# Residual projections with one 512-column product for both operand parts

## Chip, core and metric

The kernel runs on one core of a Trainium2 chip. The metric is device time in microseconds (us) for one execution; the kernel before takes 1901.9 us (median of 3 runs, 1900.17 to 1902.33).

## The reference, cut to what matters

The reference is two transformer blocks, one after the other, in float32, on a sequence of 256 tokens with 1024 channels. The first has three mixing branches, merged and projected back onto `x`; the second, of two layers, has SwiGLU feed-forward parts, an RWKV-7 time mix in layer 0, a gated MLP with a token mix in layer 1, and a memory cross-attention in each layer. Five of its matrix products end in an addition to the residual stream `x`, and these five are what the change touches:

```
x = x + merged @ w_out                      # first block        stage w_out
x = x + (y * g) @ rwkv_w_o                  # layer 0, RWKV      stage rw_o
x = x + attention_out @ xattn_wo[0]         # layer 0, memory    stage xo0
x = x + (u * sv) @ gmlp_w_o                 # layer 1, gMLP      stage gm_o (2048 rows deep)
x = x + attention_out @ xattn_wo[1]         # layer 1, memory    stage xo1
```

All weights are 1024 x 1024 but that of `gm_o`, which is 2048 x 1024. Each of the five is followed by an RMS norm of the new `x` and a projection of the result: a feed-forward part after `w_out`, `xo0` and `xo1`, the query projection of the memory attention after `rw_o` and `gm_o`.

## The kernel before

**Split precision.** TensorE multiplies in the type fp32r. So each float32 operand is held as two parts, a high one (rounded to fp32r) and a low one (the rest), and a product of weight w and activation a is three products: w high with a high, w high with a low, w low with a high (`split_mm`, L307). ScalarE makes the high part of a weight piece (`high`, L1592, recorded as L1602, tile `wh`), VectorE the low part (`low`, L2419, recorded as L2428, tile `wl`).

**Weight stream.** All weights come as one stream of 1 MB blocks, loaded by the sync engine (SP) into two raw slots; a slot is loaded again once VectorE has split both halves of it. A block is two pieces of 4 x 256 columns. There are four slots of split pieces: ScalarE writes piece p + 4 when TensorE has finished piece p (semaphore `piece_done`), and TensorE starts a piece when its low part is done (`low_done`, `piece`, L319). Each engine's order of work is written out by hand.

**Tiling.** Activations lie with channels on the 128 partitions, as 8 tiles of 256 tokens in a page of 2048 columns. A projection makes its 1024 output channels in four blocks q = 0 to 3 of two output tiles (j = 0, 1) by 256 tokens, into one PSUM bank of 512 columns. A residual projection walks over the 8 k tiles of the depth (16 for `gm_o`), four in each piece; per k and j there are three products of 256 columns, all recorded at L311. So a piece is 24 products, a block 48 (96 in `gm_o`), a stage 192 (384). In the first block TensorE waits for the operand in quarters of two k tiles (`operand_part`, L433). The banks 0 to 3 go round; `bank_free` (L325) waits until the engine that reads a bank has emptied it (`u_evac`).

**The other form.** In the SwiGLU stages the activation's two parts lie next to each other, and `wide_block` (L382) uses one product of 512 columns for w high with both parts (L398), and one of 256 columns for w low with the high part (L401), added in PSUM to the second half. Two output tiles then take two banks, and VectorE adds the two halves of a bank (L2976). In a whole piece 8 products of 512 columns are issued and then 8 of 256; behind a name's first piece they come in halves, 4 and 4.

**Around a residual stage.** VectorE's `residual` (L2519) does for each block q: split the weights of the block two ahead, wait until block q is made, add the bank to `x` (L2529; in `gm_o` L3361). For q = 3 it first makes the low quarters 0 and 1 of the next stage's operand (`late_quarters`, L2492, recorded as L2501) and a part of the norm's sum of squares (L2473, L2474), then adds block 3, then makes quarters 2 and 3. ScalarE makes the high quarters of that operand (`late_quarter`, L1678) when the blocks of `x` that it reads are added. TensorE's next stage waits for these quarters in turn.

Of the kernel before, what the change touches and what calls it, by code (L numbers as in the profile page):

```python
# [24 lines left out]
F32R = mybir.dt.float32r  # L25
# [5 lines left out]
P = 128  # L31
D = 1024
KT = D // P
T = 256
# [21 lines left out]
N_FFN = 5  # L56
AHEAD = 2
N_PAGES = 16
COL_EPS, COL_GN_EPS = 40, 41
HIDDEN_PAGES = {1: (0, 9, 10, 11, 14, 15), 2: (3, 6, 7, 8, 10, 11)}  # L60

# [11 lines left out]
for _name, _n in PARAMS:  # L73
# [16 lines left out]

SEGMENTS = [
    ("mem_k", 2, 2), ("mem_v", 2, 2), ("w_in", 40, 40), ("na_o", 4, 2), ("ca_o", 4, 2), ("hg_o", 4, 4),
    ("w_out", 4, 4), ("ffn0", 22, 33), ("ffn1", 44, 33), ("mem2_k", 4, 4), ("rw_k", 4, 4), ("mem2_u", 1, 1), ("lora", 0, 1),
    ("rw_r", 4, 5), ("lora2", 0, 1), ("mem2_v", 3, 3), ("rw_v", 4, 4), ("rw_o", 4, 4), ("xq0", 4, 4), ("xo0", 4, 4),
    ("ffn2", 44, 33), ("ffn3", 44, 33), ("gm_u", 2, 2), ("gm_v", 8, 8), ("gm_w", 6, 6), ("gm_o", 4, 8),
    ("xq1", 4, 4), ("xo1", 4, 4), ("ffn4", 44, 33),
]
W_IN_ORDER = [*range(8, 16), *range(0, 4), *range(20, 28), *range(4, 8), *range(16, 20), *range(32, 40), *range(28, 32)]
WOVEN = 18
# [76 lines left out]
def build(nc, a):  # L176

    ctx = ExitStack()
    with ctx:
        def sb(name, shape):  # L180
            return ctx.enter_context(nc.sbuf_tensor(name, shape, F32))

        t = Bag()


        def both(name, pages=1):
            at = -(-nc.sbuf_base // 32) * 32
            plain = sb(name, [P, pages * FP])
            split = [nc.alloc_sbuf_tensor_at(f"{name}_r{i}", [P, FP], F32R, offset=at + 4 * FP * i)[:, :]
                     for i in range(pages)]  # L190
# [113 lines left out]
def tensor_program(pe, t, s):  # L304
# [77 lines left out]
    def wide_block(n, bank, b, name=None, between=lambda: None):  # L382

        bank_free(n + 1)
        for hf in range(2):
# [3 lines left out]
            for run in ((0, 1), (2, 3)) if name and hf else (range(4),):  # L389
                for part in range(2):  # L390
                    for kk in run:
# [3 lines left out]
                        for j in range(2):  # L395
# [7 lines left out]
            mm.then_inc(s["piece_done"], 1)  # L403

    def token_block(n, bank, b, act, name=None):
        for hf in range(2):
# [339 lines left out]
    project("w_out", (t.page_r[11], t.page_r[10]), name="merged")  # L746


    ffn(0, "ffn0", "ffn0")
# [411 lines left out]
    project("rw_o", (t.page_r[10], t.page_r[7]), name="rw_o")  # L1161


    def memory_heads(i):
# [35 lines left out]
    def memory_attention(i, name):  # L1200
# [12 lines left out]
            turn(h)  # L1213
            mix(h - 1)
        mix(XA_H - 1)
        for k in range(4):
            n = SEG[f"xo{i}"] + k
            bank_free(n)
            for hf in range(2):
                w = piece(BLK[f"xo{i}"] + k, hf)  # L1220
                for kk in range(4):
                    c = 4 * hf + kk
                    if k == 0 and c % 2 == 0:
                        pe.wait_ge(s["att_low"], NA_H + CA_H + XA_H * i + c // 2 + 1)
                    for j in range(2):
                        mm = split_mm(ps[:, n % BANKS, j * T:(j + 1) * T],
                                      [x[:, kk * 256 + j * P:kk * 256 + (j + 1) * P] for x in w],
                                      [t.page_r[q][:, c * T:(c + 1) * T] for q in (2, 1)],
                                      start=c == 0 and j == 0, stop=c == KT - 1)
                mm.then_inc(s["piece_done"], 1)  # L1230

    memory_attention(0, "x0")
    swiglu(2, "ffn2", "ffn2")
# [37 lines left out]
    for q in range(4):  # L1271
        n, b = SEG["gm_o"] + q, BLK["gm_o"] + 2 * q
        bank_free(n)
        for k4 in range(4):
            w = piece(b + k4 // 2, k4 % 2)
            for j in range(2):
                for kk in range(4):
                    k = 4 * k4 + kk
                    if q == 0 and j == 0:
                        operand_part(f"gm{k // KT}", k % KT)  # L1280
                    mm = split_mm(ps[:, n % BANKS, j * T:(j + 1) * T],
                                  [x[:, kk * 256 + j * P:kk * 256 + (j + 1) * P] for x in w],
                                  [t.page_r[first + k // KT][:, k % KT * T:(k % KT + 1) * T] for first in (10, 7)],
                                  start=k4 == 0 and j == 0 and kk == 0, stop=k == 2 * KT - 1)
            mm.then_inc(s["piece_done"], 1)
    memory_attention(1, "x1")
    swiglu(4, "ffn4", "ffn4")
    for q in range(4):
# [106 lines left out]
def split_pair(t, first, second, m):  # L1395

    base = t.pages[:, first:first + m]
    return bass.AP(tensor=base.tensor, offset=base.offset,
                   ap=[list(base.ap[0]), [2 * m, 512 // m], [second - first + m, 2], [1, m]])


def strided_pair(t, first, second):
# [151 lines left out]
def norm_table(t, s):  # L1554
# [3 lines left out]
    rows = {  # L1558
        "mem": (t.page[0], (s["mem_in"], 16, 0), ("mem_norm", 0), t.page[1]),
        "mix0": (x, (s["x_in"], 16, 0), ("norm_mix", 0), low),  # L1560
        "ffn0": (x, (s["u_evac"], seg["w_out"] + 2, 2), ("norm_ffn", 0), h),
        "ffn1": (x, (s["x_up"], 2, 2), ("gain_fin", 0), h),
        "mix1": (x, (s["x_up"], 4 + 2, 2), ("mix_norm_2", 0), h),
        "mem2": (t.page[6], (s["mem2_in"], 16, 0), ("mem_norm_2", 0), t.page[6]),
        "x0": (x, (s["u_evac"], seg["rw_o"] + 2, 2), ("xattn_norm_2", 0), h),
        "ffn2": (x, (s["u_evac"], seg["xo0"] + 2, 2), ("ffn2_norm_2", 0), h),
        "ffn3": (x, (s["x_up"], 8 + 2, 2), ("ffn1_norm_2", 8), h),
        "mix2": (x, (s["x_up"], 12 + 2, 2), ("mix_norm_2", 8), low),
        "x1": (x, (s["u_evac"], seg["gm_o"] + 2, 2), ("xattn_norm_2", 8), h),
        "ffn4": (x, (s["u_evac"], seg["xo1"] + 2, 2), ("ffn2_norm_2", 8), h),  # L1570
        "fin2": (x, (s["x_up"], 16 + 2, 2), ("final_norm_2", 0), h),
    }
    return rows
# [839 lines left out]
def vector_program(dve, t, s):  # L2413
# [105 lines left out]
    def residual(seg, first=0, n=4, then=None):  # L2519

        for k in range(first, first + n):
            n_ = SEG[seg] + k
            if k < 3 or not then:
# [4 lines left out]
            c = slice(k * 512, (k + 1) * 512)  # L2528
            tt(t.x[:, c], ps[:, n_ % BANKS, :], t.x[:, c], ALU.add).then_inc(s["u_evac"], 1)  # L2529
            if then and k == 3:  # L2530
                late_quarters(then, (2,))

    def ffn_residual(f_, scale, then=None, after=None):
        for q in range(4):
# [818 lines left out]
            mixed_quarter(q)  # L3353
    mixed_low(7)
    for q in range(4):
        c = slice(q * 512, (q + 1) * 512)
# [4 lines left out]
        tt(t.x[:, c], ps[:, (SEG["gm_o"] + q) % BANKS, :], t.x[:, c], ALU.add).then_inc(s["u_evac"], 1)  # L3361
    late_quarters("x1", (2,))
    memory_attention(1, "ffn4", BLK["gm_o"] + 7)
    def final_part(q):
# [202 lines left out]
```

## Time and profile before

| | |
|---|---|
| runs | 1902.33, 1900.17, 1901.9 us |
| profiled execution | 1902.15 us, of which 1900.4 us span |
| TensorE products | 1856.1 us, 98%, 15872 instructions |
| weight loads | 1716.6 us, 90% |
| VectorE | 1369.4 us, 72% |
| ScalarE | 1075.6 us, 57% |
| mean granted TensorE clock | 0.998 of 2.4 GHz |
| read from HBM | 310.50 MB, 164 GB/s over the span |

The span runs from the first to the last instruction on the core. Times of products are modelled at their ends, so their starts are the ones to read: the time from one start to the next is what a product costs in a row of them.

### The profile page before, as it was taken

How to read it: one execution, taken by the hardware profiler on the slowest of the kernel's cores; microseconds unless marked ns; L12 is line 12 of the kernel's file. 1: busy time of each engine (PE TensorE's matmuls, PEld its weight loads, DVE VectorE, ACT ScalarE, POOL GpSimd, SP SyncE). 2: the span in 40 equal slices, each digit the busy share in tenths (PEclk: the TensorE clock that was granted, in tenths of full speed). 3: DMA queues.
4: the chain of work that ended last, by engine and by line, in shares of the span. 5: the costliest groups of instructions: out<-in, count | busy, mean ns of one | idle time of the engine just before them, and what ended most of it. 6: DMA issues, size and time to landing. Idle time of an engine off the chain costs nothing.

```text
span 1900.4 us, 37888 instructions
## 1 busy us (share of the span) xinstructions
PE 1856.1 (98%) x15872; PEld 1716.6 (90%) x15872; DVE 1369.4 (72%) x1808; ACT 1075.6 (57%) x1443; POOL 45.0 (2%) x42
## 2 busy tenths in 40 slices
PE   7999998999999999999998999999999999999998
PEld 7998998899998888999887998888888889998887
DVE  6687589777778877698755667766776657658764
ACT  6576576755556554468543555545554574556553
POOL 0000000000000000000142000000000000000000
PEclk9999999999999999999999999999999999999999
DMA  6844333355554455544400535554555554525553
GB/s 226 242 180 154 135 133 113 141 191 177 193 183 155 177 196 185 180 150 163 149 25 8 196 116 194 186 191 177 200 183 194 178 186 169 179 110 199 179 198 111
DMA packets 52335, 313.66 MB, mean 165 GB/s; under 512 B 13536, under 2 KB 13792, under 8 KB 14944
## 3 DMA queue, kind: packets, MB, share of 16 engines
q1 hardware_dynamic: 51760, 308.42, 45.8%
q10 hardware_dynamic: 432, 3.15, 0.4%
q8 instruction: 112, 1.84, 0.4%
q14 instruction: 31, 0.25, 0.0%
HBM read 310.50 MB, written 1.05 MB: 164 GB/s over the span
## 4 chain that ended last, share of the span: by engine, by line
PE 75%; DVE 14%; ACT 4%; issue 4%; DMA 2%; DVEq 0%; ACTq 0%; SPq 0%
PE ps L311 28%; PE ps L398 17%; PE ps L401 9%; PE ps L535 9%; DVE wl L2428 5%; PE ps L532 4%; ACT wh L1602 2%; DVE pages L2950 2%; DMA raw<-in_stream 2%; PE ps L922 1%; PE ps L937 1%; DVE pages L3050 1%; DVE pages L2516 1%; PE ps L1194 1%; DMA pages<-in_mem 0%
## 5 line engine op out<-in xcount | busy, mean ns | idle before, releaser
L2428 DVE TENSOR_TENSOR wl<-raw,wh 128x1024 fp32r<-128x1024 f32 x576 | 696.4, 1226 | 331.6 <-ACT wh L1602 327.6
L1602 ACT ACTIVATE wh<-raw 128x1024 fp32r<-128x1024 f32 x575 | 597.7, 1054 | 417.6 <-PE ps L311 143.2
L311 PE MATMUL ps<-norm_r,wh 128*128 128x256 f32 x2336 | 430.1, 285 | 0.3 <-DVE norm_r L2445 0.2
L311 PEld LDWEIGHTS ps<-norm_r,wh 128*128 128x128 f32 x2336 | 365.9, 192 | 3.3 <-issue 1.8
L311 PE MATMUL ps<-pages_r,wh 128*128 128x256 f32 x1776 | 343.8, 286 | 16.1 <-DVE wl L2428 13.7
L398 PE MATMUL ps<-norm_r,wh 128*128 128x512 f32 x1408 | 355.2, 394 | 1.9 <-DVE norm_r L2501 1.7
L311 PE MATMUL ps<-norm_r,wl 128*128 128x256 f32 x1184 | 334.9, 283 | 0.0
L311 PEld LDWEIGHTS ps<-pages_r,wh 128*128 128x128 f32 x1776 | 285.1, 193 | 20.2 <-DVE wl L2428 11.8
L398 PEld LDWEIGHTS ps<-norm_r,wh 128*128 128x128 f32 x1408 | 253.6, 189 | 47.7 <-issue 1.9
L311 PE MATMUL ps<-pages_r,wl 128*128 128x256 f32 x976 | 277.0, 284 | 0.0
L311 PEld LDWEIGHTS ps<-norm_r,wl 128*128 128x128 f32 x1184 | 227.0, 192 | 0.0
L401 PEld LDWEIGHTS ps<-norm_r,wl 128*128 128x128 f32 x1408 | 193.5, 191 | 14.2
L401 PE MATMUL ps<-norm_r,wl 128*128 128x256 f32 x1408 | 197.7, 283 | 0.0
L311 PEld LDWEIGHTS ps<-pages_r,wl 128*128 128x128 f32 x976 | 188.2, 193 | 0.0
L535 PE MATMUL ps<-pages_r,wh 128*128 128x512 f32 x704 | 177.7, 392 | 0.0
L535 PEld LDWEIGHTS ps<-pages_r,wh 128*128 128x128 f32 x704 | 126.0, 189 | 22.1
L532 PEld LDWEIGHTS ps<-pages_r,wl 128*128 128x128 f32 x704 | 97.1, 190 | 7.6
L532 PE MATMUL ps<-pages_r,wl 128*128 128x256 f32 x704 | 99.4, 282 | 0.0
L311 PE MATMUL ps<-wh,norm_r 128*128 128x512 f32 (+1 forms) x256 | 71.8, 367 | 0.0
L311 PE MATMUL ps<-work_r,wh 128*128 128x256 f32 x272 | 70.6, 284 | 0.0
L2516 DVE TENSOR_TENSOR work<-work,rstd 128x512 f32<-128x512 f32 x88 | 60.6, 689 | 9.6 <-ACT work L2095 2.9
L311 PEld LDWEIGHTS ps<-wh,norm_r 128*128 128x128 f32 x256 | 45.5, 189 | 8.8 <-issue 1.8
(341 smaller groups left out, 1918.1 us busy)
## 6 DMA issues: line engine op xcount, KB each, us to landing
raw<-in_stream SPq DMA_DIRECT2D x287, 1024.0 KB, 4.8
pages<-in_rpb SPq DMA_DIRECT2D x32, 64.0 KB, 6.2
pages<-in_mem SPq DMA_DIRECT2D x2, 512.0 KB, 6.4
raw<-in_stream SPq DMA_DIRECT2D x2, 512.0 KB, 8.1
x<-in_x SPq DMA_DIRECT2D x1, 1024.0 KB, 12.0
pages<-in_mem ACTq DMA_DIRECT2D x1, 1024.0 KB, 5.0
pages<-in_gmlp_b ACTq DMA_DIRECT2D x1, 1024.0 KB, 4.4
pages<-in_gmlp_w ACTq DMA_DIRECT2D x1, 1024.0 KB, 8.2
```

The source lines that it names most:

```text
L311: mm = pe.matmul(out, left, right, start=start and q == 0, stop=stop and q == 2, skip_group_check=True)
L398: mm = pe.matmul(ps[:, bank + j, :], wh[:, cols], t.norm_r[:, 2 * k * T:2 * (k + 1) * T], start=k == 0, stop=False, skip_group_check=True)
L401: mm = pe.matmul(ps[:, bank + j, T:2 * T], wl[:, cols], t.sq_r[:, k * T:(k + 1) * T], start=False, stop=k == KT - 1, skip_group_check=True)
L532: mm = pe.matmul(ps[:, bank, T:2 * T], w[1][:, cols], hid[:, 0:T], start=False, stop=k == HT - 1, skip_group_check=True)
L535: mm = pe.matmul(ps[:, bank, :], w[0][:, cols], hid, start=k == 0, stop=False, skip_group_check=True)
L922: mm = pe.matmul(ps[rows[1 - par], g % 2, at_:at_ + CH], level[rows[par], at_:at_ + CH], inv[rows[par], x:x + CH], start=True, stop=True)
L937: mm = pe.matmul(ps[rows[par ^ turned], bank + turned, (4 * e + u) * CH:(4 * e + u + 1) * CH], left, right, start=True, stop=True)
L1194: mm = pe.matmul(ps[:, memory_bank(i, "out", h), c * T:(c + 1) * T], t.page[15][:, at_:at_ + P], memory_turned(t, h)[:, mb * T:(mb + 1) * ...
L1602: f(t.wh[(2 * b0 + hf) % PIECE_SLOTS][:], t.raw[b0 % 2][:, hf * 1024:(hf + 1) * 1024], ACT.Copy).then_inc(s["high_done"], 1)
L2428: tt(t.wl[i][:], t.raw[b0 % 2][:, hf * 1024:(hf + 1) * 1024], t.wh[i][:].bitcast(F32), ALU.subtract).then_inc(s["low_done"], 1)
L2516: return tt(out.rearrange("p (n t) -> p n t", n=n), in_, t.rstd[:, :].unsqueeze(1).broadcast_to([P, n, T]), ALU.mult)
L2950: ins = stt(o, i_, w, o, ALU.mult, ALU.add)
```

## The change

In the five residual stages, blocks q = 0, 1 and 2 take the two-bank form. A block now uses banks n and n + 1, one for each output tile. For each k and j, one product of 512 columns has the high weight tile and both parts of the activation (its moving operand is a view of two pages, low or high part first by page number); then products of 256 columns with the low weight tile and the high part go into the second half of the bank. Block q = 3 keeps one bank and the three products of 256 columns, with j as the outer loop. VectorE adds the first halves of both banks to `x`, and behind that (it waits for its own result) the second halves; block 3 is added as before. `SEGMENTS` counts 8 banks for a stage in place of 4, and what waits for `u_evac` counts double. The pages' aliases of type fp32r are joined where a view must span two pages; no address moves.

```diff
+    def residual_piece(n, b, hf, first, pages, start, stop, ready=lambda k: None):
+        w = piece(b, hf)
+        runs = ((0, 1), (2, 3)) if first else (range(4),)
+        for run in runs:
+            for low_part in range(2):
+                for kk in run:
+                    k = 4 * hf + kk
+                    if not low_part:
+                        ready(k)
+                    for j in range(2):
+                        cols, bank = slice(kk * 256 + j * P, kk * 256 + (j + 1) * P), n % BANKS + j
+                        if low_part:
+                            mm = pe.matmul(ps[:, bank, T:2 * T], w[1][:, cols], t.page_r[pages[0]][:, k * T:(k + 1) * T],
+                                           start=False, stop=stop and k == KT - 1, skip_group_check=True)
+                        else:
+                            mm = pe.matmul(ps[:, bank, :], w[0][:, cols], both_parts(t, pages, k), start=start and k == 0,
+                                           stop=False, skip_group_check=True)
+        mm.then_inc(s["piece_done"], 1)
...
+    def residual(seg, parts, ready):
+        for q in range(4):
+            n, b = SEG[seg] + 2 * q, BLK[seg] + len(parts) * q
+            bank_free(n + 1)
+            for at_, pages in enumerate(parts):
+                for hf in range(2):
+                    start, stop = at_ == hf == 0, at_ == len(parts) - 1
+                    if q < 3:
+                        residual_piece(n, b + at_, hf, q == 0, pages, start, stop,
+                                       (lambda k: ready(KT * at_ + k)) if q == 0 else (lambda k: None))
+                    else:
+                        last_residual_piece(n, b + at_, hf, pages, start, stop)
...
+def both_parts(t, pages, k):
+    first, second = sorted(pages)
+    base = t.page_r[first][:, k * T:(k + 1) * T]
+    return bass.AP(tensor=base.tensor, offset=base.offset, ap=[list(base.ap[0]), [(second - first) * FP, 2], [1, T]])
...
-        "ffn0": (x, (s["u_evac"], seg["w_out"] + 2, 2), ("norm_ffn", 0), h),
+        "ffn0": (x, (s["u_evac"], seg["w_out"] + 4, 4), ("norm_ffn", 0), h),
...
+    def added(seg, q):
+        n, c = SEG[seg] + 2 * q, slice(q * 512, (q + 1) * 512)
+        if q < 3:
+            made, x = ps[:, n % BANKS:n % BANKS + 2, :], tiles(t.x[:, c], 2)
+            link(tt(x, made[:, :, 0:T], x, ALU.add))
+            tt(x, made[:, :, T:2 * T], x, ALU.add).then_inc(s["u_evac"], 2)
+        else:
+            tt(t.x[:, c], ps[:, n % BANKS, :], t.x[:, c], ALU.add).then_inc(s["u_evac"], 2)
```

## Rows read from the trace of the kernel before

**Rows 1.** The page's totals: busy us, share of the span, instructions.

```profile
span 1900.4 us, 37888 instructions
...
PE 1856.1 (98%) x15872; PEld 1716.6 (90%) x15872; DVE 1369.4 (72%) x1808; ACT 1075.6 (57%) x1443; POOL 45.0 (2%) x42
```

**Rows 2.** Chain of waits through stage `xo0`: start, us, engine and line, count.

```profile
1105.10 23.03 PE ps L311 x192
```

**Rows 3.** Busy us (count) of PE, PEld, DVE, ACT, POOL; PEclk, DMA share, GB/s.

```profile
380.10:403.90 23.80, 23.80 (x200) 23.80 (x200) 16.29 (x22) 11.53 (x16) 0.00 (x0) 1.00 0.52 191
1045.60:1064.00 18.40, 18.40 (x156) 18.40 (x155) 11.27 (x14) 8.64 (x12) 0.00 (x0) 1.00 0.62 232
1104.90:1127.90 23.00, 23.00 (x193) 22.97 (x193) 12.39 (x16) 10.31 (x14) 0.00 (x0) 1.00 0.33 116
...
1140.00:1180.00 40.00, 40.00 (x229) 35.14 (x229) 31.62 (x38) 23.97 (x32) 0.00 (x0) 1.00 0.55 197
600.00:603.00 3.00, 3.00 (x12) 2.61 (x12) 2.84 (x4) 0.91 (x3) 0.00 (x0) 0.50 0.00 0
```

**Rows 4.** TensorE's timeline in a SwiGLU stage: start, us (modelled end), instruction, count.

```profile
1142.38 2.00 PE L398 MATMUL ps<-norm_r,wh 128*128 128x512 f32 x8
1144.22 1.12 PE L401 MATMUL ps<-norm_r,wl 128*128 128x256 f32 x8
1145.18 2.00 PE L398 MATMUL ps<-norm_r,wh 128*128 128x512 f32 x8
...
1147.97 0.40 PE L398 MATMUL ps<-norm_r,wh 128*128 128x512 f32 x1
```

**Rows 5.** The same timeline behind `xo0`, where pieces come in halves.

```profile
1130.76 1.09 PE L398 MATMUL ps<-norm_r,wh 128*128 128x512 f32 x4
...
1132.16 1.09 PE L398 MATMUL ps<-norm_r,wh 128*128 128x512 f32 x4
...
1133.57 0.63 PE L398 MATMUL ps<-norm_r,wh 128*128 128x512 f32 x2
```

**Rows 6.** The same timeline before and in the first block of `rw_o`.

```profile
1034.14 3.70 PE L1157 MATMUL ps<-norm,const 128*128 128x512 f32 x8
1037.68 1.84 PE L317 MATMUL ps<-zrow 128*128 128x128 bf16 x30
1040.26 0.47 PE L311 MATMUL ps<-pages_r,wh 128*128 128x256 f32 x2 [0.74 <-DVE pages_r L2451]
...
1042.18 0.51 PE L311 MATMUL ps<-pages_r,wh 128*128 128x256 f32 x2 [0.27 <-DVE pages_r L2451]
...
1044.21 0.47 PE L311 MATMUL ps<-pages_r,wh 128*128 128x256 f32 x2 [0.33 <-DVE pages_r L2451]
```

**Rows 7.** VectorE's groups: the addition of two half banks; busy us, mean ns, idle.

```profile
L2976 DVE TENSOR_TENSOR work<-ps,work 128x512 f32<-128x512 f32 x44 | 30.3, 689 | 26.7 <-ACT work L2075 26.7
```

**Rows 8.** VectorE's timeline before `rw_o`: the second instruction waits for the first.

```profile
1036.76 0.69 DVE L3231 TENSOR_TENSOR pages<-pages 128x512 f32<-128x512 f32 x1 [0.19 <-ACT pages L2292]
1037.48 0.69 DVE L3232 TENSOR_TENSOR pages<-pages 128x512 f32<-128x512 f32 x1
```

**Rows 9.** VectorE's timeline in `xo0`, from the addition of block 1 on.

```profile
1118.88 0.68 DVE L2529 TENSOR_TENSOR x<-ps,x 128x512 f32<-128x512 f32 x1
1120.68 1.23 DVE L2428 TENSOR_TENSOR wl<-raw,wh 128x1024 fp32r<-128x1024 f32 x1 [1.12 <-ACT wh L1602]
...
1124.64 0.68 DVE L2529 TENSOR_TENSOR x<-ps,x 128x512 f32<-128x512 f32 x1
...
1128.17 0.69 DVE L2529 TENSOR_TENSOR x<-ps,x 128x512 f32<-128x512 f32 x1 [0.20 <-PE ps L311]
1128.78 0.87 DVE L2501 SCALAR_TENSOR_TENSOR norm_r<-x,param,norm_r 128x256 fp32r<-128x256 f32 x2
1129.84 0.88 DVE L2501 SCALAR_TENSOR_TENSOR norm_r<-x,param,norm_r 128x256 fp32r<-128x256 f32 x2 [0.19 <-ACT norm_r L1678]
```

**Rows 10.** VectorE's timeline in `gm_o`: the addition of block 3.

```profile
1641.53 0.69 DVE L3361 TENSOR_TENSOR x<-ps,x 128x512 f32<-128x512 f32 x1 [0.80 <-PE ps L311]
```

More of the change, by code:

```diff
@@ L58 @@
 N_PAGES = 16
+ALIASES = [(0, 1), (1, 2), *((i, 1) for i in range(3, 7)), (7, 5), *((i, 1) for i in range(12, N_PAGES))]
 COL_EPS, COL_GN_EPS = 40, 41
@@ L92 @@
     ("mem_k", 2, 2), ("mem_v", 2, 2), ("w_in", 40, 40), ("na_o", 4, 2), ("ca_o", 4, 2), ("hg_o", 4, 4),
[L93 to L96, printed above, removed]
+    ("w_out", 8, 4), ("ffn0", 22, 33), ("ffn1", 44, 33), ("mem2_k", 4, 4), ("rw_k", 4, 4), ("mem2_u", 1, 1), ("lora", 0, 1),
+    ("rw_r", 4, 5), ("lora2", 0, 1), ("mem2_v", 3, 3), ("rw_v", 4, 4), ("rw_o", 8, 4), ("xq0", 4, 4), ("xo0", 8, 4),
+    ("ffn2", 44, 33), ("ffn3", 44, 33), ("gm_u", 2, 2), ("gm_v", 8, 8), ("gm_w", 6, 6), ("gm_o", 8, 8),
+    ("xq1", 4, 4), ("xo1", 8, 4), ("ffn4", 44, 33),
 ]
@@ L188, in both @@
             plain = sb(name, [P, pages * FP])
-            split = [nc.alloc_sbuf_tensor_at(f"{name}_r{i}", [P, FP], F32R, offset=at + 4 * FP * i)[:, :]
-                     for i in range(pages)]
+            split = []
+            for first, n in ALIASES if pages > 1 else ((0, 1),):
+                alias = nc.alloc_sbuf_tensor_at(f"{name}_r{first}", [P, n * FP], F32R, offset=at + 4 * FP * first)
+                split += [alias[:, i * FP:(i + 1) * FP] for i in range(n)]
             return plain, split
@@ L403, in wide_block, with last_residual_piece @@
             mm.then_inc(s["piece_done"], 1)
+    def residual_piece(n, b, hf, first, pages, start, stop, ready=lambda k: None):
[16 more added lines that the diff above has]
+        mm.then_inc(s["piece_done"], 1)
+    def last_residual_piece(n, b, hf, pages, start, stop):
+        w = piece(b, hf)
+        for j in range(2):
+            for kk in range(4):
+                k = 4 * hf + kk
+                mm = split_mm(ps[:, n % BANKS, j * T:(j + 1) * T], [x[:, kk * 256 + j * P:kk * 256 + (j + 1) * P] for x in w],
+                              [t.page_r[q][:, k * T:(k + 1) * T] for q in pages],
+                              start=start and j == 0 and kk == 0, stop=stop and k == KT - 1)
+        mm.then_inc(s["piece_done"], 1)
+    def residual(seg, parts, ready):
[10 more added lines that the diff above has]
+                        last_residual_piece(n, b + at_, hf, pages, start, stop)
     def token_block(n, bank, b, act, name=None):
@@ L745, in tensor_program @@
     project("hg_o", (t.page_r[6], t.page_r[13]), name="hg")
-    project("w_out", (t.page_r[11], t.page_r[10]), name="merged")
+    residual("w_out", ((11, 10),), lambda k: operand_part("merged", k))
     ffn(0, "ffn0", "ffn0")
@@ L1160, in tensor_program @@
     idle_products(4, 30)
-    project("rw_o", (t.page_r[10], t.page_r[7]), name="rw_o")
+    residual("rw_o", ((10, 7),), lambda k: operand_part("rw_o", k))
     def memory_heads(i):
@@ L1215, in memory_attention, with ready @@
         mix(XA_H - 1)
[L1216 to L1230, printed above, removed]
+        def ready(c):
+            if c % 2 == 0:
+                pe.wait_ge(s["att_low"], NA_H + CA_H + XA_H * i + c // 2 + 1)
+        residual(f"xo{i}", ((2, 1),), ready)
     memory_attention(0, "x0")
@@ L1270, in tensor_program @@
         mix_quarters(MIX_BEHIND[k - 1])
[L1271 to L1285, printed above, removed]
+    residual("gm_o", ((10, 7), (11, 8)), lambda k: operand_part(f"gm{k // KT}", k % KT))
     memory_attention(1, "x1")
@@ L1564, in norm_table @@
         "mem2": (t.page[6], (s["mem2_in"], 16, 0), ("mem_norm_2", 0), t.page[6]),
-        "x0": (x, (s["u_evac"], seg["rw_o"] + 2, 2), ("xattn_norm_2", 0), h),
-        "ffn2": (x, (s["u_evac"], seg["xo0"] + 2, 2), ("ffn2_norm_2", 0), h),
+        "x0": (x, (s["u_evac"], seg["rw_o"] + 4, 4), ("xattn_norm_2", 0), h),
+        "ffn2": (x, (s["u_evac"], seg["xo0"] + 4, 4), ("ffn2_norm_2", 0), h),
         "ffn3": (x, (s["x_up"], 8 + 2, 2), ("ffn1_norm_2", 8), h),
         "mix2": (x, (s["x_up"], 12 + 2, 2), ("mix_norm_2", 8), low),
-        "x1": (x, (s["u_evac"], seg["gm_o"] + 2, 2), ("xattn_norm_2", 8), h),
-        "ffn4": (x, (s["u_evac"], seg["xo1"] + 2, 2), ("ffn2_norm_2", 8), h),
+        "x1": (x, (s["u_evac"], seg["gm_o"] + 4, 4), ("xattn_norm_2", 8), h),
+        "ffn4": (x, (s["u_evac"], seg["xo1"] + 4, 4), ("ffn2_norm_2", 8), h),
         "fin2": (x, (s["x_up"], 16 + 2, 2), ("final_norm_2", 0), h),
@@ L2517, in scaled, with residual @@
                   t.rstd[:, :].unsqueeze(1).broadcast_to([P, n, T]), ALU.mult)
[L2519 to L2523, printed above, removed]
+    def added(seg, q):
[6 more added lines that the diff above has]
+            tt(t.x[:, c], ps[:, n % BANKS, :], t.x[:, c], ALU.add).then_inc(s["u_evac"], 2)
+    def residual(seg, then):
+        for k in range(4):
+            if k < 3:
                 low(BLK[seg] + k)
@@ L2527, in residual @@
             dve.wait_ge(s["piece_done"], 2 * (BLK[seg] + k) + 2)
[L2528 to L2531, printed above, removed]
+            added(seg, k)
+        late_quarters(then, (2,))
     def ffn_residual(f_, scale, then=None, after=None):
@@ L3355, in vector_program @@
     for q in range(4):
-        c = slice(q * 512, (q + 1) * 512)
         lows("gm_o", 2 * q, 2 if q < 3 else 1)
@@ L3360, in vector_program @@
         dve.wait_ge(s["piece_done"], 2 * (BLK["gm_o"] + 2 * q) + 4)
-        tt(t.x[:, c], ps[:, (SEG["gm_o"] + q) % BANKS, :], t.x[:, c], ALU.add).then_inc(s["u_evac"], 1)
+        added("gm_o", q)
     late_quarters("x1", (2,))
```

## The prediction

> **What bounds the kernel now.** I read the page's totals first, then the chain of waits inside one of the five stages that change, then busy time by stretch, then that stage's VectorE timeline. In the totals TensorE is busy 98% of the span and weight loads 90% [rows 1]. That alone does not name the limit of a stage, so the chain is asked for the second residual projection of the memory attention: from its first product to the next stage it is one piece, 192 products in 23.03 us, with no other engine in it [rows 2]. So a product of 256 columns costs 23.03 / 192 = 120 ns, and everything else in that stage lies under TensorE. The stretches say the same of the other stages, of which three stand in the rows and the two others are alike: TensorE is busy in all of each stretch, VectorE in 54 to 68% of it, the DMA engines in 33 to 62%, and the granted clock is 1.00 [rows 3]. The reader is to see there that 1 us taken from TensorE's stream in such a stage is 1 us of the time, as long as whoever feeds the next stage does not become late.
>
> **What the change removes.** A block has two pieces (half blocks), each with 4 k tiles and 2 output tiles: 8 triples of 256-column products. The new piece has 8 products of 512 columns and 8 of 256. The columns streamed are the same (6144 a piece); 8 products and 8 weight loads go. Before, a piece is 24 x 0.120 = 2.88 us. The kernel already holds pieces of the new form, in the wide blocks of the SwiGLU stages: two in a row start at 1142.38, 1145.18 and 1147.97, so one is 5.59 / 2 = 2.795 us [rows 4]. A whole piece therefore gains 0.085 us. The first block of a stage is issued in halves (4 + 4 products, for two k tiles); the same form stands at 1130.76, 1132.16 and 1133.57, 1.405 us a half, 2.81 us a piece [rows 5], a gain of 0.07 us.
>
> Pieces: four stages have three changed blocks of two pieces (2 in halves, 4 whole); the gMLP output, with twice the depth, has 12 (4 in halves, 8 whole). Together 12 x 0.07 + 24 x 0.085 = 0.84 + 2.04 = 2.88 us. In the first block of the RWKV output TensorE waits three times for VectorE's operand quarters, at 1040.26, 1042.18 and 1044.21 [rows 6]. What it gains in the first two quarters (0.035 us each) is waited away: 0.07 us less. Sum: 2.8 us.
>
> The Trainium skill (TensorE: Matmul & The Clock Gate, section Back-to-back issue gap) gives a product its columns at the clock and a constant of about 2.5 ns. By that rule, as an estimate, a triple would save one constant, and 288 triples 0.7 us. The trace doesn't agree: 120 ns for 256 columns [rows 2] and 230 ns for 512 (1142.38 to 1144.22, eight of them) [rows 4] save 2 x 120 - 230 = 10 ns a triple.
>
> One thing no row shows: the new 512-column operand is two runs of 256 from two pages, where the wide blocks read one run. Bounds: if the jump is free, 230 ns; if each run pays as a product of its own, 2 x 120 = 240 ns, and the gain is nil. Further out stand the 512-column products of plain fp32, 8 from 1034.14 to 1037.68, 442 ns each [rows 6]. I take 230: the nearest row has the same width, type and weights, and only one jump in 512 columns is new. Below 230 I see no reason.
>
> **What it adds on VectorE.** Three blocks of a stage get a second addition: 15 in all. A two-bank addition in this view is in the trace 44 times at 689 ns [rows 7], as long as the old one. The first of the pair is waited for by the second; such a pair starts 1037.48 - 1036.76 = 0.72 us apart [rows 8]. So each block costs VectorE 0.72 us more, 10.8 us in all. After blocks 0 and 1 of a stage it lies in an idle time of 1.12 us before the next weight split (L2428 at 1120.68 after block 1; after block 0 the same) [rows 9], so it costs nothing. Without that cover it would delay a split whose piece TensorE reaches only three pieces later.
>
> After block 2 it counts. Behind that addition, in VectorE's order, stand the low quarters 0 and 1 of the next operand, a part of the norm's sum, block 3's addition, then quarters 2 and 3, for which TensorE's next stage waits. In the memory attention's stage VectorE was free for block 3's addition 0.20 us before 1128.17 [rows 9]. Block 2 now ends 2 x 0.07 + 4 x 0.085 = 0.48 us earlier, and with it the split and the addition. So VectorE is free at 1128.17 - 0.20 - 0.48 + 0.72 = 1128.21, 0.04 us later than before on the clock. Quarter 2, ready before at 1128.78 + 0.87 = 1129.65, is ready at 1129.69. TensorE needs it at the first half of the second piece, 1130.76 [rows 5], now 0.48 earlier: 1130.28. The cover shrinks from 1.11 to 0.59 us and holds. Quarter 3 is needed 1.40 us later and is ready 1.07 us later: 0.92 left. The other stages have the same 0.20 us or more; in the gMLP output VectorE idles 0.80 us there [rows 10] and TensorE's block ends 0.96 us earlier, so the addition still waits for TensorE.
>
> **What it adds in waits.** A changed block takes two of four banks, so block 2 waits for block 0's additions, block 3 for block 1's, and the next stage's first wide block for block 2's. Worked out in the same stage: block 1's additions end at 1118.88 - 0.31 + 1.40 = 1119.97 (0.31 is the gain of two blocks), and block 3 starts at 1105.10 + 17.28 - 0.48 = 1121.90 [rows 2, 9]. That is 1.9 us of room; block 0 to 2 has 1.8, block 2 to the next stage 1.9. Nothing on TensorE stands still for it. Weights, DMAs and the q = 3 block keep their instructions; SP's loads move earlier with the splits, and the DMA share of at most 0.62 [rows 3] has room.
>
> **Sum.** The profiled execution: 1902.15 us, 1900.4 span and 1.75 around it. 1902.15 - 2.8 = 1899.35. It stood 0.25 above the median of the runs shown (1901.9), so the forecast is **1899.1 us**. That is 0.15%; a measurement of this kernel tells about 0.2%, 3.8 us, from no change.
>
> **The rivals.**
> - Only columns count, or each run of the operand pays as a product: 8 x 240 + 8 x 120 is the old 2.88 us a piece, gain nil, 1901.9. For it: equal columns, and no row of a two-run operand. Against: rows 4. Chance 0.14.
> - Slower: the two-run operand costs more than two products. It decides from 240 ns on; from 253 ns it is slower by 0.2% (288 x 0.013 = 3.8 us). At 260 ns it costs 288 x 0.020 = 5.8 us, 1907.7. For it: only that no row excludes it, with 442 ns as the far end [rows 6]. Against: every 512-column product of this type in the trace runs at 230. Chance 0.07.
> - The hand-over becomes late: if the additions out of two half banks took 1.23 us each (the split's duration [rows 9]), VectorE would be late by another 1.1 us, 0.51 past the cover. In four stages that is 2.0 us, leaving 0.8: 1901.1. Against: rows 7. Chance 0.07.
> - Weight loads are the limit, and each of the 288 removed frees 120 ns: 34.6 us, 1867.3. For it: 90% in [rows 1] and loads in all of each stage's time [rows 3]. The Trainium skill (Perfetto Trace Analysis, section Identifying the Most-Contended Engine) judges TensorE by weight-load share rather than by matmul share. Against: with a third fewer loads the wide piece still takes 2.795, not 16 x 0.120 = 1.92 us, and in its stretch loads take 35.14 of 40 us [rows 3, 4]. Chance 0.05.
>
> One further risk is inside the range: the granted clock was 0.50 from 600 to 603 us, after a wait of TensorE [rows 3]. Such a stretch falling elsewhere, or not at all, moves the time by a microsecond or two.
>
> **How the numbers follow.** The forecast has 0.67. Its own range is 1898.0 to 1900.6, by the spread of the runs before (1900.17 to 1902.33); some 0.12 of the 0.67 falls under 1898.1, which is 0.2% faster. The range for 8 in 10 reaches over the two cases without much gain: 1897.3 to 1902.4. Faster by over 0.2%: 0.12 + 0.05 = 0.17. Slower: 0.07. Within: 0.76.
>
> **What would show it.** In the profile after: 512-column products of the new lines 230 ns apart; a whole changed piece 2.80 us and a stage of four blocks 0.48 us shorter (gMLP 0.96); 15 more additions of 0.69 us, each 0.72 behind its first half; VectorE idle before block 3's addition near zero in four stages; TensorE's next stage starting without a wait for quarter 2 or 3. The prediction is wrong if the two-run product is 240 ns or more, or if a wait of TensorE for the normalised operand (L2501) appears behind a residual stage.

## The result: 0.1 to 0.2% slower, and the profile after

The changed kernel took 1906.6 us in the median of eight runs (1902.3 to 1907.5), beside 1901.7 for the kernel before on the same chip: ratio 1.0019, 95% interval [1.0010, 1.0028]. Eleven more runs, on another occasion, gave 1903.5 us (1901.8 to 1907.2): ratio 1.0010 [1.0001, 1.0019]. The forecast was 1899.1, with 1897.3 to 1902.4 for 8 in 10: both medians lie outside, and the sign is wrong.

First the page of the changed kernel: span, and busy us, share and instructions of each engine.

```profile
span 1904.4 us, 37347 instructions
...
PE 1852.1 (97%) x15584; PEld 1700.3 (89%) x15584; DVE 1379.1 (72%) x1823; ACT 1075.6 (56%) x1443; POOL 45.1 (2%) x42
```

288 products and 288 weight loads are gone and 15 additions have come; TensorE is busy 4 us less than in [rows 1], yet the span is 4 us longer. So the time was lost where TensorE is idle. Before looking there, the changed stage itself, which answers [rows 2]: the chain of waits of the changed kernel through `xo0` (start, us, engine and line, count).

```profile
1111.14 0.93 PE ps L424 x4
...
1116.73 1.84 PE ps L424 x8
1118.57 0.95 PE ps L421 x8
1119.52 1.84 PE ps L424 x8
...
1127.90 5.76 PE ps L314 x48
1133.66 1.84 PE ps L401 x8
...
1136.45 0.93 PE ps L401 x4
```

The 512-column products over two pages (L424) are 230 ns each, the 256-column ones (L421) 119; a whole changed piece is 1119.52 - 1116.73 = 2.79 us, three changed blocks take 1127.90 - 1111.14 = 16.76 us instead of 3 x 5.76 = 17.28. Nothing but TensorE is in the chain. The next rows answer [rows 9]: VectorE's timeline at the end of the same stage.

```profile
1130.17 0.68 DVE L2555 TENSOR_TENSOR x<-ps,x 128x512 f32<-128x512 f32 x1
1130.96 0.69 DVE L2556 TENSOR_TENSOR x<-ps,x 128x512 f32<-128x512 f32 x1
...
1134.21 0.69 DVE L2558 TENSOR_TENSOR x<-ps,x 128x512 f32<-128x512 f32 x1
1134.81 0.88 DVE L2532 SCALAR_TENSOR_TENSOR norm_r<-x,param,norm_r 128x256 fp32r<-128x256 f32 x2
1135.88 0.88 DVE L2532 SCALAR_TENSOR_TENSOR norm_r<-x,param,norm_r 128x256 fp32r<-128x256 f32 x2 [0.19 <-ACT norm_r L1709]
```

The halves are added 0.79 us apart (forecast 0.72), block 3's addition has no idle time ahead of it, quarter 2 is ready at 1134.81 + 0.88 = 1135.69, and TensorE comes to it at 1136.45. So the stage goes as forecast (the cover of quarter 2 is 0.76 us, forecast 0.59). What was not forecast stands in the RWKV stage, which the change does not touch: TensorE's waits from 930 to 1050 us (line, releaser, us in total, times, longest), first the kernel before, then the changed one.

```profile
PE ps L1096 <- issue: 1.4, 1, 1.4
PE ps L311 <- DVE pages_r L2451: 1.3, 3, 0.7
PE ps L1029 <- issue: 1.1, 2, 0.8
PE ps L937 <- issue: 1.1, 1, 1.1
PE ps L922 <- issue: 1.0, 4, 0.3
...
```

```profile
PE ps L970 <- issue: 3.4, 5, 2.3
PE ps L1144 <- issue: 2.7, 2, 1.4
PE ps L985 <- issue: 2.3, 2, 1.3
PE ps L424 <- DVE pages_r L2482: 1.0, 2, 0.7
...
PE ps L1077 <- issue: 0.3, 1, 0.3
...
```

"issue" is time in which the engine waited for nothing that the profile shows. It was 4.6 us before (L1096, L1029, L937, L922) and is 8.7 us after, in the same code (L922 has become L970, L937 L985, L1096 L1144). The longest, in the changed kernel's timeline:

```profile
988.59 0.24 PE L970 MATMUL ps<-pages,norm 64*64 64x64 f32 x1
991.11 0.86 PE L970 MATMUL ps<-pages,norm 64*64 64x64 f32 x23 [2.29 <-issue]
```

What happens in it is in the DMA view of 988 to 992 us (queue, kind: packets, MB, share of 16 engines):

```profile
q1 hardware_dynamic: 32, 0.13, 8.0%
q8 instruction: 1, 0.02, 1.4%
```

A block of instructions is fetched: one transfer of 16,384 bytes, 256 instructions of 64 bytes, on a queue of its own. I took every such fetch of TensorE's queue from the trace, and every gap above 0.65 us between the starts of two products from 924 us to `rw_o`, and counted where the product behind the gap stands in TensorE's program (its place modulo 256). Listed are the gap's end, its length, the time from the start of the last fetch to that end (us), and the place.

```
before    924.16 0.97  4.67  (waits for wl)
          956.85 1.27  2.34  203    1008.43 1.04  2.39  205    1033.17 1.61  2.41  205
changed   925.99 0.96 24.80  (waits for wl)
          959.64 1.54  2.36  203     991.11 2.52  2.21  204     995.10 1.18  2.39  205
         1036.85 1.55  2.36  205    1040.33 1.60  2.34  205
```

But for the wait for a low weight tile at 924, every gap ends 2.2 to 2.4 us after a fetch began, and stands at places 203 to 205: a place that comes once in 256 instructions. I take it for the boundary where one block ends and the next begins. (It need not be place 0: the count starts at the kernel's first instruction, and that need not start a block.) They sum to 3.92 us before and 8.39 after, 4.47 more; the stage itself (from the 36 idle products ahead of it to the 30 ahead of `rw_o`, whose rows follow for the changed kernel) takes 198.65 us instead of 194.05: 4.60 more.

```profile
845.49 2.18 PE L320 MATMUL ps<-zrow 128*128 128x128 bf16 x36
...
1044.14 1.84 PE L320 MATMUL ps<-zrow 128*128 128x128 bf16 x30
```

In the kernel before these are 843.63 (a row like the first) and 1037.68 [rows 6].

### The profile page after: what moved, and what is told of

Same layout as the page of the kernel before. It is cut to its first block, busy times and chain, and to the rows that moved or that the text cites. A ratio compares the mean times of both kernels' runs of the same rounds, so it can differ in the third digit from the quotient of the medians.

```text
span 1904.4 us, 37347 instructions
## 1 busy us (share of the span) xinstructions
PE 1852.1 (97%) x15584; PEld 1700.3 (89%) x15584; DVE 1379.1 (72%) x1823; ACT 1075.6 (56%) x1443; POOL 45.1 (2%) x42
## 4 chain that ended last, share of the span: by engine, by line
PE 72%; DVE 15%; ACT 5%; issue 4%; DMA 3%; DVEq 0%; SPq 0%; ACTq 0%
PE ps L314 20%; PE ps L401 17%; PE ps L404 9%; PE ps L583 9%; DVE wl L2459 6%; PE ps L580 4%; PE ps L424 3%; DMA raw<-in_stream 3%; ACT wh L1633 2%; PE ps L421 2%; DVE pages L2988 2%; PE ps L970 1%; PE ps L985 1%; DVE pages L3088 1%; PE ps L1242 1%
## 5 line engine op out<-in xcount | busy, mean ns | idle before, releaser
L314 PE MATMUL ps<-pages_r,wh 128*128 128x256 f32 x1200 | 239.2, 287 | 16.8 <-DVE wl L2459 15.9
L314 PEld LDWEIGHTS ps<-pages_r,wh 128*128 128x128 f32 x1200 | 195.1, 193 | 20.1 <-DVE wl L2459 14.1
L314 PE MATMUL ps<-pages_r,wl 128*128 128x256 f32 x688 | 195.5, 284 | 0.0
L583 PE MATMUL ps<-pages_r,wh 128*128 128x512 f32 x704 | 177.7, 392 | 0.0
L583 PEld LDWEIGHTS ps<-pages_r,wh 128*128 128x128 f32 x704 | 126.0, 189 | 22.1
L314 PEld LDWEIGHTS ps<-pages_r,wl 128*128 128x128 f32 x688 | 132.9, 193 | 0.0
L580 PEld LDWEIGHTS ps<-pages_r,wl 128*128 128x128 f32 x704 | 97.1, 190 | 7.6
L580 PE MATMUL ps<-pages_r,wl 128*128 128x256 f32 x704 | 99.4, 282 | 0.0
L424 PE MATMUL ps<-pages_r,wh 128*128 128x512 f32 x288 | 75.0, 395 | 1.4 <-DVE pages_r L2482 1.4
```

The source lines that it names most:

```text
L314: mm = pe.matmul(out, left, right, start=start and q == 0, stop=stop and q == 2, skip_group_check=True)
L424: mm = pe.matmul(ps[:, bank, :], w[0][:, cols], both_parts(t, pages, k), start=start and k == 0, stop=False, skip_group_check=True)
L580: mm = pe.matmul(ps[:, bank, T:2 * T], w[1][:, cols], hid[:, 0:T], start=False, stop=k == HT - 1, skip_group_check=True)
L583: mm = pe.matmul(ps[:, bank, :], w[0][:, cols], hid, start=k == 0, stop=False, skip_group_check=True)
```

## The experiments

**Theory 1 (places).** TensorE's instructions come in blocks of 16,384 bytes. The 48 products that leave `w_out` are 96 instructions (a weight load and a product each), so all the code behind lies 96 places earlier against the block boundaries. The RWKV stage's dense small products meet the boundaries at worse points. **Theory 2 (the additions).** VectorE's additions, the waits for banks or the transfers that start earlier cost it. **Theory 3 (chance).** The clock and the transfers vary from run to run; nothing of the kernel is behind it.

The Trainium skill (Runtime: NRT & Kernel Launch, section Instruction fetch mechanics) tells of such blocks: 16 KiB, 256 instructions, which the sequencer fetches over a DMA queue of its own while it runs the one before. By it 96 places are three eighths of a block; the traces agree with the size (16,384 bytes a fetch).

Each trace is divided at the two rows of idle products shown above: A is the time up to the first, B the RWKV stage between them, C the rest of the span. Differences are against the profiled run of the kernel before (843.63, 194.05, 862.72 us).

| kernel | median us | ratio, 95% interval | A, us | B, us | C, us |
|---|---|---|---|---|---|
| changed | 1906.6 | 1.0019 [1.0010, 1.0028] | +1.86 | +4.60 | -2.46 |
| changed, again (e5) | 1903.5 | 1.0010 [1.0001, 1.0019] | -0.17 | +5.68 | -2.51 |
| before, moved by 160 (e1) | 1907.3 | 1.0031 [1.0020, 1.0043] | +2.05 | +4.20 | -0.05 |
| before, moved by 256 (e2) | 1914.4 | 1.0067 [1.0053, 1.0081] | +14.51 | -0.32 | -0.09 |
| changed, moved back by 96 (e3) | 1898.6 | 0.9981 [0.9972, 0.9990] | -0.59 | +0.18 | -2.49 |
| four later stages alone (e4) | 1899.3 | 0.9990 [0.9981, 0.9999] | -0.02 | -0.03 | -2.55 |
| `w_out` alone (e6) | 1906.4 | 1.0023 [1.0014, 1.0033] | +0.23 | +4.98 | -0.01 |
| changed, 96 waits in one place (e7) | 1908.0 | 1.0030 [1.0018, 1.0042] | +8.36 | -0.23 | -2.53 |
| changed, loops on block starts (e8) | 1904.1 | 1.0011 [1.0002, 1.0020] | -0.89 | +5.33 | -2.54 |
| changed, 84 idle products (e9) | 1899.2 | 0.9987 [0.9978, 0.9996] | -1.50 | +0.55 | -1.25 |
| changed, 68 idle products (e10) | 1899.4 | 0.9989 [0.9980, 0.9998] | -1.62 | +0.71 | -2.49 |
| changed, 100 idle products (e11) | 1902.6 | 1.0008 [0.9999, 1.0017] | -2.31 | +2.90 | -1.99 |
| before, 164 idle products (e12) | 1904.8 | 1.0016 [1.0006, 1.0025] | -0.45 | +2.32 | -0.07 |

**e1, e2: the code moved, without the change.** Two fulfilled waits ahead of a product of `w_out` add one instruction.

```diff
+    def pad():
+        for _ in range(min(1, pads[0])):      # e2: min(2, pads[0])
+            pe.wait_ge(s["consts_in"], 16)
+            pe.wait_ge(s["ones_in"], 16)
+            pads[0] -= 1
...
+            pad()                             # in split_mm, ahead of each product
...
+    pads[0] = 160                             # e2: 256
     project("w_out", (t.page_r[11], t.page_r[10]), name="merged")
```

> The kernel before, with the whole computation as it was, and 160 waits that are long fulfilled put between the products of the w_out stage on TensorE's queue: the TensorE program behind w_out then lies at the same places of its 16 KB fetch blocks as in the changed kernel. Theory 1 (the changed kernel lost its time because its TensorE code lies otherwise against the fetch blocks, above all in the RWKV stage): slower than before by 3 to 6 us, 1905 to 1908 us, and TensorE's waits for nothing in that stage grow from some 3.5 us to 8 us. Theory 2 (the added work of VectorE, the banks and the operand handed over cost it): the same as before within 1 us. Theory 3 (chance of the clock and of the transfers, nothing of the kernel): the same as before within 1 us.

> The kernel before with 256 such waits in the w_out stage, which is one whole fetch block: the code behind it lies where it lay against the blocks. It shows what the waits themselves cost. Theories 1, 2 and 3 all say the same as before, within 0.7 us; were it slower by 3 us, the first experiment would say nothing of places.

The two rows of e1 (the first pair) and of e2:

```profile
845.68 2.18 PE L326 MATMUL ps<-zrow 128*128 128x128 bf16 x36
1043.93 1.84 PE L326 MATMUL ps<-zrow 128*128 128x128 bf16 x30
...
858.14 2.18 PE L326 MATMUL ps<-zrow 128*128 128x128 bf16 x36
1051.87 1.84 PE L326 MATMUL ps<-zrow 128*128 128x128 bf16 x30
```

e1 is slower by 5.4 us with the old computation. Some 1.5 us of that fall in `w_out` itself, where the waits were added (24.51 us from its first product to the next stage's, instead of 23.04); the 4.20 us of B, where nothing was added, are what theory 1 says. Its gaps are four of the changed kernel's five (960.13, 991.32, 1036.64, 1040.11; 2.36 to 2.41 us after a fetch began, places 203 to 205). They sum to 6.23 us, 2.3 more than before. The rest of the 4.20 is in the windows behind the gap at 991.32 (busy TensorE us and count, granted clock, DMA share, GB/s):

```profile
990.00:992.00 2.00, 0.68 (x15) 0.86 0.00 0
992.00:994.00 2.00, 2.00 (x44) 0.50 0.04 8
994.00:996.00 2.00, 2.00 (x84) 0.78 0.00 0
```

The granted clock is 0.50, the lower of the two levels (1.2 GHz), in the middle window, and in parts of the two beside it: 2 x (0.14 + 0.50 + 0.22) = 1.7 us are lost there. The trace of the changed kernel itself shows no such stretch in this stage; that of e5 does, behind its gap at 957.89:

```profile
958.00:960.00 2.00, 1.64 (x35) 0.68 0.00 0
960.00:962.00 2.00, 2.00 (x47) 0.50 0.00 0
962.00:964.00 2.00, 2.00 (x132) 0.97 0.00 0
```

e8 has such a stretch too, behind a gap of 3.03 us (granted clock 0.62 from 990 to 992 us, 0.52 from 992 to 994). So in three traces a gap was followed by a second toll; the traces of the changed kernel and of e6, with gaps of up to 2.5 us, have none, and what decides it was not tested. Of the first eight runs of the changed kernel the four with a mean clock of 0.996 took 1907.0 to 1907.5 us.

e2 missed: it should have been as fast as before and was 12.5 us slower. The three parts show why it still serves: all of it is in A, where two added instructions a product were more than the stage hides, and the stage that is moved by one whole block keeps its time (-0.32). The prediction for the stage holds, the one for the sum fell.

**e3, e4, e6: moved back, and the change in parts.** e3 puts 96 such waits into the changed `w_out`. e4 and e6 compute the named stages as before and add their blocks once:

```diff
+APART = ('w_out',)                            # e6: ('rw_o', 'xo0', 'gm_o', 'xo1')
...
-                    if q < 3:
+                    if seg in APART:
+                        plain_piece(...)      # triples of 256-column products in one bank
+                    elif q < 3:
                         residual_piece(...)
...
-        if q < 3:
+        if q < 3 and seg not in APART:
             made, x = ps[:, n % BANKS:n % BANKS + 2, :], tiles(t.x[:, c], 2)
```

> The changed kernel with 96 such waits in its w_out stage: these fill the place of the 96 TensorE instructions that the change took out there, so that all from the end of w_out to rw_o (the RWKV stage among it) lies in the fetch blocks as before. Theory 1: the RWKV stage takes its old time and the sum comes out at 1898 to 1901 us, faster than before by 1 to 4 us. Theory 2: as the changed kernel, 1905 to 1907.5 us. Theory 3: anywhere between, without a shift of the RWKV stage.

> The change in rw_o, xo0, gm_o and xo1 alone; w_out computes as before (12 products of 256 columns a piece pair, one add a block). Theory 1: the RWKV code isn't moved, so 1898 to 1901 us, about 2 us faster than before. Theory 2: four fifths of the loss stay, some 1904 to 1906 us.

> The change in w_out alone; rw_o, xo0, gm_o and xo1 compute as before. It has the gain of one stage of five (some 0.5 us) and moves the RWKV code by the same 96 instructions as the whole change. Theory 1 (places): some 1905 to 1908 us, the loss in full and hardly any gain. Theory 2 (the additions in each of the five stages): a fifth of the loss, 1901 to 1903 us.

All three came as theory 1 has it. The two rows of e3, then TensorE's waits in its stage from 930 to 1050 us:

```profile
843.04 2.18 PE L329 MATMUL ps<-zrow 128*128 128x128 bf16 x36
...
1037.27 1.84 PE L329 MATMUL ps<-zrow 128*128 128x128 bf16 x30
```

```profile
PE ps L434 <- DVE pages_r L2494: 1.4, 3, 0.7
PE ps L1156 <- issue: 1.3, 1, 1.3
PE ps L997 <- issue: 1.3, 1, 1.3
PE ps L1089 <- issue: 1.1, 2, 0.8
PE ps L982 <- issue: 1.0, 4, 0.3
...
```

That is the list of the kernel before, line by line, to within 0.2 us. With every addition of the change in place, and 96 instructions that do nothing, the kernel is 3.2 us faster than before instead of 1.4 to 4.9 slower. And `w_out` alone, one of the five stages, has the whole loss (B +4.98) and none of the gain behind (C -0.01): theory 2 falls. Theory 3 falls with it: B is longer in the changed kernel, e1 and e6, where the stage's code lies 96 places off, and as before in e2, e3 and e4, where it lies as before. The rows of e6:

```profile
843.86 2.18 PE L321 MATMUL ps<-zrow 128*128 128x128 bf16 x36
...
1042.89 1.84 PE L321 MATMUL ps<-zrow 128*128 128x128 bf16 x30
```

**e5: the changed kernel again.**

> The changed kernel once more, for a second trace and more times. If its stalls belong to the code's places, the RWKV stage has the same gaps on TensorE (some 1.5, 2.5, 1.2, 1.6 and 1.6 us) at the same products, and the time is 1902 to 1907.5 us again. If they came by chance, they lie elsewhere. The gap of 1.5 us at the start of the first SwiGLU stage (before the 448th us), which the first shifted copy of the kernel before did not have, should be gone if it was a chance of the transfers.

Of the five gaps three are back at the same products, two with the same length (2.52 and 1.18) and one longer (1.81 for 1.54); of the two at the stage's end there is one, of 1.87. The median is 3 us lower than the first time. The gap at the start of the first SwiGLU stage was 1.5 us and is 0.9; e6 has it at 1.5, e1, e3 and e4 not above 0.65. It is no part of the stage, and what makes it is open.

**e7: the 96 waits in one place.** They stand ahead of mem2_u's first product.

```diff
+    for _ in range(96):
+        pe.wait_ge(s["consts_in"], 16)
+        pe.wait_ge(s["ones_in"], 16)
     project("mem2_u", mem2, n=1, token=True)
```

> The changed kernel with 96 fulfilled waits in one place, ahead of mem2_u's first product, where TensorE waits 1.5 to 1.8 us for a low weight tile in every trace. The RWKV code lies as before, w_out and the first two SwiGLU stages as in the changed kernel. Theory 1: 1897 to 1899.5 us, somewhat under the copy with the waits in w_out, since these waits should lie in a wait that is there. Theory 2: 1905 to 1907 us.

The stage keeps its old time (B -0.23), as theory 1 says, and the sum is a miss by 9 us: A is 8.36 us longer. The waits don't fit into the 1.5 us that TensorE stands there; the gap is 8.67 us long, 7.2 more for 96 instructions, 75 ns each, and the granted clock is 0.57 from 840 to 850 us, in its second half and behind it.

**e8: both loops on block starts.**

```diff
+    pe.addr_align(256, offset=0, max_nops=0)
     with pe.Fori(0, last - 1) as i:
         next_level(0, i, i + 1)
```

> The changed kernel with the first instruction of each of the RWKV stage's two TensorE loops (some 395 instructions each) put on the start of a fetch block, so that each loop lies in two blocks; the code behind them moves with them. Theory 1: the two gaps at the second loop's start and back edge (2.5 and 1.2 us) go, that in the first loop (1.5 us) may; what the straight code behind does isn't known. 1897 to 1904 us. Theory 2: 1905 to 1907 us.

The gaps inside the loops went, and two of 2.73 and 3.03 us came at the loops' entries (953.95 and 989.94, 2.8 us after a fetch began): the program jumps over padding there, and the loop's first instruction comes 2.53 and 2.84 us after the jump. The time is that of the changed kernel (1904.1, between what theory 1 and theory 2 gave), so this run decides nothing between them. Aligning a loop is no gain if the jump to it waits for the same fetch.

**e9 to e12: places without added waits.** The 36 idle products ahead of the stage become more and smaller ones.

```diff
-    idle_products(7, 36)
+    idle_products(7, 84, rows=64, cols=64)    # e10: 68, cols=80; e11: 100, cols=48; e12 (before): 164, cols=32
```

> The changed kernel; the 36 idle products of 128 columns that TensorE runs ahead of the RWKV stage while it waits for operands become 84 smaller ones (64 columns of weights, 64 moving), which fill about the same 2.5 us with 96 more instructions. The RWKV code lies in its fetch blocks as in the kernel before, and no wait is added to a stage that has work. Theory 1 (places): the RWKV stage takes some 195.7 us from the first idle product to rw_o, as before, not 200 to 201; the sum 1897 to 1899.5 us. Theory 2 (the additions): 1903 to 1907 us.

> As the run with 84, with 68 idle products (80 columns): the RWKV code lies 32 instructions ahead of its place of before. Both loops then still lie as they did (the first in three blocks, the second in two). Theory 1, if the loops decide: 1897 to 1900 us, as with 84; if the straight code decides, another time, up to 1904 us. Theory 2: 1903 to 1907 us.

> As the run with 84, with 100 idle products (48 columns): the RWKV code lies 32 instructions behind its place of before; the first loop in three blocks, the second in two, as before. Theory 1, if the loops decide: 1897 to 1900 us; if the straight code decides, another time, up to 1904 us. Theory 2: 1903 to 1907 us.

> The kernel before with 164 small idle products (64 columns of weights, 32 moving) in place of the 36: 256 instructions more, one whole fetch block, so the places are those of before. It mends the control whose waits cost 14 us. Theories 1 and 2: the RWKV stage within 0.5 us of before; the sum within 1 us of before unless 164 products take longer than the wait that they fill, and then by that excess, which the trace shows ahead of the stage's first weight product.

e9 and e10 are faster than both kernels, e9 with the places of before, e10 32 instructions ahead of them. In e11, 32 behind it, a gap of 1.61 us appears in the second loop and B is 2.90 us longer, of which 1.2 is the idle products themselves (3.35 us for 2.18). The expectation had the loops wrong, since it took the blocks to begin at place 0. With the boundary at 204, where the gaps are, the second loop (397 instructions) touches two blocks in the kernel before, e3, e4, e9 and e10, and three in the changed kernel, e1, e6 and e11. The first five have no gap in it, the others one or two, so that loop decides there. It is no rule for loops: the first loop touches three blocks in most of these kernels and two in e11, and in all of them but e8 it has one or two gaps of 0.9 to 1.8 us. And the second loop's gaps do not stand at its back edge, as the expectation of e8 has it, but at block boundaries within its first pass; from one pass to the next it is 0.45 to 0.67 us in every trace, whatever the places. While the changed kernel's loops run their second and third passes (960.4 to 968.8 and 996.8 to 1007.3 us) no fetch begins and no gap above 0.65 us stands: the three blocks of such a loop are not fetched again. e12, the control with a whole block, is slower by 3 us; its 164 idle products take 5.37 us instead of 2.18 in these two rows, and B less that excess is 0.9 us under before:

```profile
843.18 5.37 PE L317 MATMUL ps<-zrow 128*64 128x32 bf16 x164
...
1039.55 1.84 PE L317 MATMUL ps<-zrow 128*128 128x128 bf16 x30
```

e9's C falls 1.2 us short of the others': TensorE waits once, at 1329 us, for VectorE in the third SwiGLU stage, which no other of these traces does; why is open.

## Why the prediction was wrong

**What the change removes: right for the stages, but not all that it removes.** C holds four of the five stages. Their gain by the forecast's terms is 2.8 - 0.48 = 2.3 us; seven traces of the change, with the RWKV code in its old place or not, show 2.46 to 2.55 (e9 and e11 less). The gain of `w_out` shows in the stage itself: 22.55 us to the next stage's first product instead of 23.04, 0.49 us (forecast 0.48). In A it is hidden by the start of the program: A varies from -2.3 to +1.9 us between six traces whose code is the same up to there (changed, e5, e8 to e11), and `w_out`'s first product starts at 379.2 to 382.5 us in all the traces, with the same code ahead of it. e4 measured 1899.3 us, e3 1898.6, beside the forecast of 1899.1.

**What it adds on VectorE, what it adds in waits: right.** No wait of TensorE for banks or for the operand's quarters appeared behind a residual stage.

**The step that failed is the one of the products that go: "8 products and 8 weight loads go" was priced in the stage they leave, and nowhere else.** The sentence "Weights, DMAs and the q = 3 block keep their instructions" is true, and not enough: they keep the instructions, not the places. The missing term is +4.6 us (+5.7 where the clock fell as well) in a stage 500 us later. With it the sum is -2.8 + 4.6 = +1.8 us, 1903.7, beside 1903.5 and 1906.6 measured. That it meets the second median so well is in part luck (the profiled run there has 5.68 in B); in the first, the profiled run has 1.86 us more in A, and four of eight runs a lower clock. The prediction gave 0.76 to a change of less than 0.2%, and both medians are that; this too is luck, since a gain of its size and a larger loss that it did not have came together.

It could have been read in the trace of before: that stage already had 4.6 us of TensorE waiting for "issue", in four groups of waits, and its gaps ended 2.3 to 2.4 us after an instruction fetch. A stage that waits there is a stage whose time hangs on where its code lies, and every edit ahead of it that adds or takes instructions moves that code.

**The rivals.** The two-run operand costs no more than one run (230 ns). The hand-over was in time. Weight loads were not the limit. The risk named, a half-speed stretch "falling elsewhere", did come in e1, e5 and e8, each time right behind a gap; the profiled run of the changed kernel has none in the stage that it lost in. No rival had the mechanism that decided.

**Why this stage and not the changed ones.** In the changed kernel the straight code of the stage runs such products:

```profile
1033.80 0.44 PE L1144 MATMUL ps<-norm,pages 64*64 64x64 f32 x16
1034.03 0.44 PE L1144 MATMUL ps<-pages 64*64 64x64 f32 x16
```

16 of them in 0.23 us are 14 ns each. At two instructions a product, 16,384 bytes (128 products) last 1.8 us, an estimate from these rows: less than the 2.2 to 2.4 us from a fetch's start to the end of the gap. 256-column products at 120 ns make a block last 15 us, and no stage of those shows such a gap. The Trainium skill (Runtime: NRT & Kernel Launch, section Instruction fetch mechanics) calls the crossing of a block boundary mostly hidden; for these products the traces differ (3.9 us of gaps before, 8.4 after). The Trainium skill says there also that a taken branch to a block that isn't there stalls; e8's two jumps over padding agree, with 2.53 and 2.84 us.

**Why these boundaries and not their neighbours.** TensorE's program in the changed kernel, loops taken once, touches 111 blocks, and the trace has 110 fetches: none for the first two blocks, one for each that follows, and one more at the end. So, taken in order, each boundary can be laid beside the start of its fetch, in every trace but e8's, whose padding is not in the count. These are 1435 boundaries, and behind none does the first product start less than 2.16 us after the fetch began. All gaps above 0.65 us at a boundary end 2.2 to 2.9 us after it, but the one that e7's waits make. At neighbours without a gap TensorE arrives no sooner than that: in the changed kernel at 1014.81 and 1018.91, 2.45 and 2.50 us after the fetch, without a stop. So a boundary costs what is still missing of some 2.2 to 2.9 us when the products of the block ahead have run out.

**Left open.** Which place is best was sampled at few shifts. What sets the moment at which a fetch begins is not known: in the changed kernel's stage, mostly 0 to 2.4 us after the first product of the block ahead. No run changed the fetch itself; that "issue" is the wait for it rests on the places of the gaps (203 to 205 in the changed kernel, e1, e3, e6 and e9 alike), on the times from the fetch's start, and on their going when the code moves back.

## What to carry to other kernels

Look for waits marked "issue" in stages of many small products before pricing an edit far ahead of them: such a stage can gain or lose more by its place than the edit gives. Count the gaps' places modulo 256 and lay the gaps beside the fetches: if the places are all the same and the gaps end at the same time after a fetch's start, it points to the fetch. When a small gain fails, restore the place with as many idle instructions as went, in a stretch with slack, before blaming the edit; here that turned a loss into the forecast gain. Look at the filler's own price: in `w_out` a single added instruction a product cost nothing for 96 products of the changed kernel (e3, 22.55 us) and 1.5 us for 160 of the old one (e1), two a product cost 14 us (e2), and 96 in a row 7 us (e7).

## What the runs showed of the hardware

- A gap at a block boundary ends 2.2 to 2.9 us after the fetch began, although the transfers ahead of these gaps take 0.9 to 1.4 us.
- Two loops of 395 and 397 instructions, each touching three blocks, ran their second and third passes without a fetch (changed kernel).
- A fulfilled wait that stands alone takes TensorE's sequencer some 75 ns (96 in 7.2 us).
- A product whose moving operand jumps once between two pages takes 230 ns for 512 columns, like one over a single page.
- Idle products of 64 columns of weights and 32 moving take 5.37 / 164 = 33 ns each, as those of 64 and 48 do (3.35 / 100): smaller ones are not faster.
